# Moving squares and low-part subtracts between VectorE, ScalarE and GpSimd in a differential-attention kernel

## What is computed

```python
def probs(qb, k):
    s = jnp.einsum('bhqd,bhkd->bhqk', qb, k).astype(jnp.float32) * scale + bias
    return jax.nn.softmax(jnp.where(mask, s, -jnp.inf), axis=-1)
w = probs(q1b, k1) - lam * probs(q2b, k2)
return jnp.einsum('bhqk,bhkd->bhqd', w.astype(v.dtype), v)
...
o_da = diff_attention(dq[0], dq[1], dk[0], dk[1], dv, rel_bias, lam)
o_da = rms_norm(o_da, subln_g[l]) * (1.0 - lambda_init)
...
o_sb = stick_breaking(to_heads(sq), to_heads(sk), to_heads(sv))
o_sb = rms_norm(o_sb, sb_out_g[l])
...
x = x + jnp.concatenate([o_da, o_sb], axis=-1) @ w_o[l]
```

## Time and profile before

| | us |
|---|---|
| median of 3 runs | 1433.49 |
| the profiled execution | 1435.44 |
| its span | 1433.70 |
| TensorE busy | 1386.6 (97%) |
| VectorE busy | 619.8 (43%) |
| ScalarE busy | 444.1 (31%) |
| GpSimd busy | 59.3 (4%) |

### The profile page before, as it was taken

How to read it: one execution, slowest core, us unless ns; L and a number is a source line. 1 busy time by engine, 2 the same in 40 slices (tenths; PEclk the granted TensorE clock), 3 DMA queues, 4 the chain that set the end, 5 groups by cost and what they waited for, 6 DMA issues and landing times.

```text
span 1433.7 us, 16158 instructions
## 1 busy us (share of the span) xinstructions
PE 1386.6 (97%) x6524; PEld 871.9 (61%) x6524; DVE 619.8 (43%) x1104; ACT 444.1 (31%) x755; POOL 59.3 (4%) x113
## 2 busy tenths in 40 slices
PE   6999999899999999999999999999999999999998
PEld 5777775576533333333333375655678888888886
DVE  5225555835434334433343465487353232233224
ACT  4124775623010010001200263386353222223232
POOL 0000110000210001001000001000000000000000
PEclk9999999899999999999999999999999999999999
DMA  8541117618899999999999923000053313313001
GB/s 350 219 170 59 59 60 294 264 59 333 320 424 425 424 423 424 424 428 425 421 424 427 374 74 147 1 1 1 0 235 117 118 59 117 117 59 118 30 0 59
DMA packets 32371, 304.07 MB, mean 212 GB/s; under 512 B 6315, under 2 KB 6315, under 8 KB 10536
## 3 DMA queue, kind: packets, MB, share of 16 engines
q1 hardware_dynamic: 29592, 298.69, 51.6%
q0 software_dynamic: 2272, 3.52, 0.7%
q10 hardware_dynamic: 432, 0.81, 0.2%
HBM read 302.59 MB, written 4.25 MB: 214 GB/s over the span
## 4 chain that ended last, share of the span: by engine, by line
PE 86%; DMA 8%; DVE 3%; ACT 2%; issue 1%; DVEq 0%; SPq 0%; POOL 0%; ACTq 0%
PE ps L58 81%; DMA ring<-in_w 7%; PE ps L1291 2%; PE ps L1011 1%; PE ps L967 1%; DMA MORE<-in_w_gu 1%; DMA X<-in_x 0%; PE ps L678 0%; PE ps L698 0%; PE ps L880 0%; ACT WH L1856 0%; PE ps L926 0%; ACT TO L1574 0%; DVE TMP L2190 0%; DVE TMP L1974 0%
## 5 line engine op out<-in xcount | busy, mean ns | idle before, releaser
L58 PE MATMUL ps<-ring,B 128*64 128x512 f32 (+3 forms) x624 | 146.8, 589 | 2.4 <-DMA ring<-in_w 1.2
L58 PE MATMUL ps<-XH,WH 128*128 128x512 f32 (+1 forms) x368 | 140.6, 382 | 1.3 <-DVE XL L1971 0.7
L58 PE MATMUL ps<-XL,WH 128*128 128x512 f32 (+1 forms) x368 | 139.8, 380 | 0.0
L58 PE MATMUL ps<-XH,WL 128*128 128x512 f32 (+1 forms) x368 | 139.7, 380 | 0.0
L1633 ACT ACTIVATE TMP<-ps 64x512 f32<-64x512 f32 x32 | 19.0, 594 | 302.7 <-PE ps L58 301.6
L58 PE MATMUL ps<-B 128*64 128x512 f32 (+5 forms) x408 | 110.2, 555 | 0.3 <-DMA B<-in_w 0.3
L2307 DVE TENSOR_TENSOR X<-ps,X 128x512 f32<-128x512 f32 x112 | 72.2, 686 | 63.7 <-PE ps L58 63.7
L58 PEld LDWEIGHTS ps<-ring,B 128*64 128x64 f32 (+1 forms) x624 | 43.7, 137 | 78.0 <-issue 73.8
L1856 ACT ACTIVATE WH<-ring 128x2048 fp32r<-128x2048 f32 x24 | 46.0, 1918 | 126.3 <-PE ps L58 126.3
L1971 DVE TENSOR_TENSOR WL<-ring,WH 128x2048 fp32r<-128x2048 f32 x24 | 55.0, 2292 | 66.2 <-ACT WH L1856 66.2
L58 PE MATMUL ps<-ring,TMP 128*64 128x512 f32 x336 | 75.3, 594 | 5.0 <-DMA ring<-in_w 5.0
(11 more groups left out here) (365 smaller groups left out, 2442.5 us busy)
## 6 DMA issues: line engine op xcount, KB each, us to landing
ring<-in_w SPq DMA_DIRECT2D x57, 2048.0 KB, 26.9
B<-in_w SPq DMA_DIRECT2D x21, 2048.0 KB, 27.8
ring<-in_w_ada SPq DMA_DIRECT2D x12, 2048.0 KB, 8.4
MORE<-in_w SPq DMA_DIRECT2D x11, 2048.0 KB, 25.4
ring<-in_w_gu SPq DMA_DIRECT2D x8, 2048.0 KB, 8.0
TO<-in_w SPq DMA_DIRECT2D x7, 2048.0 KB, 18.9
ring<-in_w_in SPq DMA_DIRECT2D x6, 2048.0 KB, 12.2
ring<-in_w_down SPq DMA_DIRECT2D x4, 2048.0 KB, 7.3
```

The source lines that it names most:

```text
L58: return e.matmul(o, l, r, start=first, stop=last, skip_group_check=True)
```

## The change

The squares of the attention rows go from VectorE to ScalarE, where they stand at the head of `od_rms`, four instructions each waiting for the one before. The four subtracts `so_low` and the first two of the eight `wo_low` go to GpSimd, behind its selects. `wo_low` keeps units 2 to 7 on VectorE.

```diff
 def gpsimd(e):
...
+        for m in range(4):
+            e.wait_ge(so_hi, m + 1)
+            e.tensor_tensor(OLS[:, m, :], oT[:, m, :], OHS[:, m, :], ALU.subtract).then_inc(so_lo, 1)
+        for n in range(2):
+            h, u = WO[n]
+            hi, lo = (x[n % 2][:, :].rearrange("p (c n) -> p c n", c=2) for x in (UH, UL))
+            e.wait_ge(wo_hi, n + 1)
+            e.tensor_tensor(lo, slot(I_WO + h, 8, 512)[:, 2 * u:2 * u + 2, :], hi, ALU.subtract).then_inc(wo_lo, 1)
         e.wait_ge(si_set, 1)
...
         def od_rms(n):
             r = slice(12 - 4 * n, 16 - 4 * n)
+            e.wait_ge(od_out, n + 1)
+            for q, g in enumerate(range(12 - 4 * n, 16 - 4 * n)):
+                if n or q:
+                    e.wait_ge(od_sq, 4 * n + q)
+                e.activation(jk, odv[:, g, :], ACT.Square, accum_out=sso[:, g:g + 1]).then_inc(od_sq, 1)
             e.wait_ge(od_sq, 4 * n + 4)
...
-        def so_low(m):
-            e.wait_ge(so_hi, m + 1)
-            minus(OLS[:, m, :], oT[:, m, :], OHS[:, m, :]).then_inc(so_lo, 1)
-
-        def od_squares(n):
-            e.wait_ge(od_out, n + 1)
-            for g in range(12 - 4 * n, 16 - 4 * n):
-                q = 4 * n + g - (12 - 4 * n)
-                if q:
-                    e.wait_ge(od_sq, q)
-                e.tensor_tensor_reduce(jk, odv[:, g, :], odv[:, g, :], 1.0, 0.0, ALU.mult, ALU.add, sso[:, g:g + 1]).then_inc(od_sq, 1)
...
         def wo_low(n):
+            if n < 2:
+                return
...
-            if i in (5, 7, 10, 12):
-                so_low((5, 7, 10, 12).index(i))
...
-            if i in (6, 10, 14):
-                od_squares((i - 6) // 4)
...
-            if i in (13, 15):
-                wo_low((i - 13) // 2)
         od_low(1)
-        od_squares(3)
         od_low(2)
```

## The result

The changed kernel takes **1439.83 us** in the median (1435.97 to 1441.32, 11 runs), the kernel before 1433.74 (1431.26 to 1435.22, 11 runs on the same chip). The ratio is 1.0040, 95% interval 1.0032 to 1.0047: slower by 5.7 us, with ends at 4.6 and 6.7. The profiled execution took 1439.85 us, its span 1437.8, against 1435.44 and 1433.70 of the one before. The changed kernel's runs fall in two groups: four at 1435.97 to 1437.64 us with a mean granted clock of 0.997 or 0.998, and seven at 1439.55 to 1441.32 with 0.993 to 0.995; the profiled execution is one of the second.

A forecast was written before the change was run, and what follows sets the result against it. TensorE, busy 97%, bounds the kernel, with ScalarE the path in steps 7 and 11. 1.76 + 1.76 - 0.4 + 1.1 = +4.2 us gives 1439.6 profiled, 1437.7 us as median; range 1433.5 to 1440.2.

The forecast's parts named there:

- The path: Attention loop, steps 7 and 11: ScalarE holds TensorE, so squares added there delay the kernel one for one.
- Squares, 0.44 us each: Four groups of four on ScalarE: 1.76 us a group, +1.76 each in steps 7 and 11.
- The 0.4 that was to come back at step 13: ScalarE's 0.44 us wait for VectorE's maxima before 277.27 goes away: -0.4 us.
- Groups 2 and 3: Squares in step 15 and after the loop: 0 each, covered by 2.26 and 1.85 us.
- 1.85 us of cover: After the loop, from L2097's end at 294.29 to TensorE's turn at 296.14, to cover group 3's 1.76 us.
- Clock: One more low stretch behind step 8's wait, grown from 1.13 to 2.9 us: +1.1 us, bounds 0 and 1.8.
- D: Rival: additions stand, but the low stretch of 280 to 290 ends early or does not come: 1433.5 us, chance 0.13.
- the sum: 1.76 + 1.76 - 0.4 + 1.1 = +4.2 us, on the profiled execution's 1435.44 us.
- Low parts and units, 0: Four stick-breaking low parts and two map units on GpSimd cost 0; units at the upper price +1.0 us.
- rival B: Unit 0's low part comes late (GpSimd slow, or it and VectorE hold each other up): +5.2, 1438.7 us, chance 0.10.
- 1.95 lower: Median shown, 1433.49 us, against the profiled execution; the offset took the forecast from 1439.6 to 1437.7 us.
- rival A: The additions stand, with no further low clock stretch: +3.1, 1436.6 us, chance 0.25.

The follow-up runs named there:

- the reordered kernel: Kernel before with ScalarE's and VectorE's loop steps in another order and nothing on GpSimd: 1430.97 us, ratio 0.9983.
- the last run: Reordered kernel with reordered tail and later VectorE low parts, the change's squares on ScalarE at steps 8, 14, 16 and after the loop: 1430.41 us, ratio 0.9978.

## Why the prediction was right, and where not

1437.7 us was forecast, 1439.8 measured, slower as forecast and inside the range. Point by point:

**The path.** That ScalarE and not VectorE holds TensorE in steps 7 and 11 is shown by the squares put in other steps (-3.3 us) and doubled (+8.05 us against the changed kernel, 7.7 by the ratios), and by the reordered kernel, which gains without any engine doing less.

**Squares, 0.44 us each.** Measured 0.43, so 1.72 for four. Step 8's matmul came 1.69 us later where 1.76 was forecast. Its wait came out at 3.15, not 2.9, because TensorE also arrived 0.3 us earlier, at 257.25 against 257.58. Step 12's wait was forecast at 2.1 and was 2.14. The 0.4 that was to come back at step 13 did: ScalarE's exponentials there no longer wait, step 12 is 5.64 us late and step 14 5.17. Groups 2 and 3 cost nothing in the profile. The copy behind group 2 was done at 290.04, 0.28 us before TensorE used it at 290.32, and no wait stands before the turn of 300.06. Group 3's norm, L2098, began at 299.02 and took 0.69, so 0.35 us of the 1.85 us of cover were left; a second set of squares showed at once.

**Clock, the term that was mis-sized.** +1.1 was taken for one more low stretch, with 1.8 as its upper end. Between step 8 and step 10 TensorE fell back 3.62 - 1.69 = 1.93 us, a little over that end: the low stretch reached over the product into the step behind it. The second product took 0.54 more. Filled waits returned 1.9 us in the median. The ground for the term was weak as well: it compared 2.9 us with the 2.07 that had brought a fall, but in the profiles of two other kernels (low parts and units on GpSimd; squares in other steps) the same 2.07 us brought none. Against it stood something that was a rival of its own (D) and came in part: over the first output products the clock was 0.83, not 0.69, and from the first output product to the last turn 4.86 - 3.92 = 0.94 us came back. The forecast had counted nothing for this. It about cancels what the low stretches cost beyond 1.1 us, and that the sum met the profile to 0.1 us is luck in this part.

**Low parts and units, 0.** In the full change right, as no TensorE wait for either engine stands there, and removing the GpSimd half from it did not change the time (1439.77 against 1439.83). But the 0 held only because the squares make TensorE too late to meet VectorE's stall, which the forecast had not worked out. GpSimd's prices were 1.27 and 2.35 us, inside the bounds and near the 2.4 that was taken. The step that failed is its reason. The estimate asked when GpSimd's result is wanted, and only rival B asked what GpSimd does to VectorE beside it, and there only as a late low part. Alone, this half costs 1.7 us, and it is no late result: VectorE stands. The rows of 274.94 and 270.21 end 0.01 and 0.02 us after the GpSimd subtract beside them. The Trainium skill (SBUF — State Buffer, "Summary: rules for kernel authors") says that when a VectorE instruction has two SBUF inputs and a GpSimd instruction reads SBUF, the one that is issued second fully blocks until the first finishes; these two rows agree. Rival B had left open how the two hold each other up, and looked only at the low part.

**From the profiled execution to the median.** The sum against the profiled execution, +4.2, met +4.1 of span. The median was taken to be 1.95 lower, since the profiled execution of before was. The changed kernel's profiled execution lay at its median, 1439.85 to 1439.83, so 1437.7 came out 2.1 too low. It lies between the two groups of runs of the changed kernel. The lower one, 1435.97 to 1437.64 at the higher mean clock, is 3.0 us over the kernel before by its median, 1436.8, and so where rival A was (+3.1, no further low stretch); the forecast's nearness to the median of all runs is in part luck. A profile shows one execution, and an offset from one kernel's profile cannot be carried to another whose clock falls more often. What decides on a run's group was not tried, and the trace shows a run of the higher group only.

## What to carry to other kernels

Before moving work off a full engine, look for who ends the waits of the engine that bounds the kernel; here VectorE was full and ScalarE was late, so unloading the one onto the other lost 5.9 us while another order of ScalarE's and VectorE's steps won 2.7, and two more reordered places another 2.7. A small instruction can be dear: price a move to GpSimd by what VectorE has to do with two SBUF inputs while it runs, and keep it to stretches where nobody waits for VectorE. And where the sum is made on one profiled run, compare it with that run, not with a median scaled from it.

## What the runs showed that was not expected

- GpSimd's subtracts shut VectorE out. A VectorE instruction with two SBUF inputs that began beside a GpSimd subtract ended 0.01 to 0.02 us after it in all five cases of the changed kernel, 0.31 to 1.30 us long in place of 0.22. Instructions with an input in PSUM, or with one input, ran through beside it at their usual length (in the run with low parts and units alone, the reciprocal of 274.75: 0.16 us). A square on VectorE that reads one SBUF tensor as both inputs was held too (0.29 us alone, 1.35 at 267.33 with the four rows on GpSimd). The other way round the runs show little: a GpSimd subtract that began while such a VectorE instruction ran took 1.32 us in place of 1.27 (271.09 in the changed kernel).
- The length of a wait alone did not tell whether the clock falls. Behind the same wait of 2.07 us it fell in the kernel before (product 3.06 us) and not with the low parts and units on GpSimd (1.92). In the last run TensorE waited 3.18 us before 280.57 and the stretch behind it was granted full speed:

```profile
280.00:290.00 10.00, 9.43 (x49) 7.88 (x50) 5.43 (x11) 7.14 (x30) 0.00 (x0) 1.00 0.01 2
```

  whereas in the reordered kernel before, with a wait of 1.77 us before 272.42, it was 0.66 over 270 to 280:

```profile
270.00:280.00 10.00, 7.93 (x34) 5.64 (x33) 9.42 (x46) 7.87 (x28) 0.00 (x0) 0.66 0.40 163
```
